# Three output-product stages of a two-layer transformer: weights staged in idle buffers, first tile evicted and multiplied between the weights' roundings

## What is computed

```python
# am, first attention layer
mixed = concat([rmsnorm(out_a, g_out_a), rmsnorm(out_b, g_out_b)])   # (1024, 1024)
x1 = x + mixed @ w_out                                             # (1024, 1024) @ (1024, 1024)
# em, retention and stick-breaking layer
mixed = concat([group_norm(ret) * silu(gate), stick * silu(gate)])
x3 = x2 + rms_norm(mixed @ even_w_out, post_norm)
# om, recurrent layer
mixed = concat([group_norm(hc) * silu(gate), lru_out])
out = x3 + rms_norm(mixed @ odd_w_out, post_norm)
```

## Time and profile before

| | |
|---|---|
| median of 3 runs | 2683.31 us (2678.47 to 2697.49) |
| the profiled execution | 2682.25 us, its span 2680.4 us |
| busy share of the span | PE 82%, PEld 68%, DVE 49%, ACT 39%, POOL 20% |
| mean granted TensorE clock | 0.899 |
| the eight weight pieces sent by SP (first and last issue) | am 700.5 to 712.6, em 1929.3 to 1954.0, om 2554.5 to 2566.6 |
| product's matmuls (first and last start) | am 725.9 to 824.6, em 1968.2 to 2066.9, om 2579.8 to 2671.3 |

### The profile page before, as it was taken

How to read it: one execution, slowest core, us unless ns; L and a number is a source line. 1 busy time by engine, 2 the same in 40 slices (tenths; PEclk the granted TensorE clock), 3 DMA queues, 4 the chain that set the end, 5 groups by cost and what they waited for, 6 DMA issues and landing times. The chain is left out here.

```text
span 2680.4 us, 34378 instructions
## 1 busy us (share of the span) xinstructions
PE 2210.9 (82%) x12244; PEld 1824.7 (68%) x12244; DVE 1314.9 (49%) x2225; ACT 1032.4 (39%) x1828; POOL 542.4 (20%) x658
## 2 busy tenths in 40 slices
PE   7996897999596699995599997688568899945658
PEld 5885897999584566663488885577557778834547
DVE  3334675555453666763632112577555434336743
ACT  3333554555331455552421100355343333246532
POOL 1003103421010212221200004234312000036622
PEclk9998998999797799998799997788879899977779
DMA  4777765321345399983833212332252442141142
GB/s 148 216 226 212 239 197 135 95 64 42 130 134 208 135 368 365 351 335 127 297 129 114 79 47 91 85 71 47 73 171 95 150 145 99 62 125 41 41 173 95
DMA packets 216721, 399.15 MB, mean 149 GB/s; under 512 B 90513, under 2 KB 111377, under 8 KB 203905
## 3 DMA queue, kind: packets, MB, share of 16 engines
q1 hardware_dynamic: 177008, 314.52, 37.1%
q10 hardware_dynamic: 28384, 61.62, 6.1%
q0 software_dynamic: 11184, 21.13, 2.2%
HBM read 300.16 MB, written 114.85 MB: 155 GB/s over the span
## 5 line engine op out<-in xcount | busy, mean ns | idle before, releaser
L78 PE MATMUL pe_acc<-pe_w,hT 128*128 128x512 f32 x960 | 222.5, 393 | 0.0
L78 PEld LDWEIGHTS pe_acc<-pe_w,hT 128*128 128x128 f32 x960 | 181.8, 190 | 37.8
L78 PE MATMUL ex_gu<-hT,ex_xT 128*128 128x512 f32 x792 | 194.4, 401 | 0.8 <-DVE hT L2321 0.8
L2321 DVE TENSOR_TENSOR hT<-ex_raw,hT 128x2048 fp32r<-128x2048 f32 x66 | 150.9, 2287 | 88.8 <-ACT hT L2292 88.8
L78 PE MATMUL pg_acc<-hT,pg_w 128*128 128x512 f32 x768 | 179.6, 395 | 8.6 <-DVE pg_w L257 8.6
L78 PEld LDWEIGHTS pg_acc<-hT,pg_w 128*128 128x128 f32 x768 | 145.2, 189 | 42.1 <-DVE pg_w L257 9.6
L78 PEld LDWEIGHTS ex_gu<-hT,ex_xT 128*128 128x128 f32 x792 | 147.5, 190 | 34.5 <-DVE hT L2321 1.2
L2292 ACT ACTIVATE hT<-ex_raw 128x2048 fp32r<-128x2048 f32 x66 | 126.2, 1914 | 42.4 <-PEq L47 23.9
L1697 PE MATMUL ab_op<-ab_v,ab_pT 128*128 128x64 f32 x1024 | 121.3, 272 | 0.0
L296 DVE COPY pe_o<-pe_acc 128x512 f32<-128x512 f32 x28 | 19.3, 691 | 206.6 <-PE pe_acc L78 206.5
L2250 PE MATMUL ex_dn<-ex_wd,ex_hT 128*128 128x512 f32 x264 | 118.7, 592 | 0.8 <-ACT ex_hT L2286 0.8
(11 more groups left out here) (461 smaller groups left out, 5056.0 us busy)
## 6 DMA issues: line engine op xcount, KB each, us to landing
ex_raw<-in_w_gate SPq DMA_DIRECT2D x33, 1024.0 KB, 7.7
ex_raw<-in_w_up SPq DMA_DIRECT2D x33, 1024.0 KB, 11.7
ex_wd<-in_w_down SPq DMA_DIRECT2D x33, 1024.0 KB, 14.2
pe_raw<-in_even_w_in SPq DMA_DIRECT2D x6, 2048.0 KB, 9.2
pg_raw<-in_odd_w_in SPq DMA_DIRECT2D x5, 2048.0 KB, 9.3
scr_q<-pa_o SPq DMA_DIRECT2D x32, 256.0 KB, 4.1
scr_k<-pa_o SPq DMA_DIRECT2D x32, 256.0 KB, 3.8
hT<-scr_k SPq DMA_DIRECT2D x16, 512.0 KB, 6.5
```

Source lines behind the costliest of these rows:

```text
L78: mm = pe.matmul(out, a(p, k), b(q, k), start=(k == 0 and i == 0), stop=(k == n - 1 and i == 2))
L2321: dve.tensor_tensor(split(s, LO)[:, :, g, :], raw[:, s % NW, g, :].rearrange("p (k n) -> p k n", k=8), split(s, HI)[:, :, g, :].bitcast(F3 ...
```

## The change

`mix_out` gets a list `pieces` of up to eight staging buffers: `raw`, then the back's two `xs`, then the back's two `z`. That gives NR = 8 in am, 6 in em (raw has two there) and 6 in om (there is no `z`). SP sends the rows of tile 0, then NR weight pieces without a wait, then the rows of tile 1, then what is left of the weights behind waits for the LO roundings. ACT evicts tile 0 between the sixth and the seventh rounding. DVE makes the LO parts of pieces 1 and 2 ahead of `dve_z(0)`, those of 3 to 5 behind it, then `dve_turn(0)`, then 6 to 8. PE multiplies tile 0's first half (24 matmuls) piece by piece as the LO parts come, with the turn of tile 0 ahead of the first piece that needs it, then turns tile 1, then the second half. In om the pieces are taken in the order 4, 5, 6, 7, 0, 1, 2, 3. The number of instructions of each kind is the same.

```diff
@@ -744,7 +744,7 @@
                     r.pe_turn(pe, t)
 
 
-def mix_out(nc, name, ident, hT, w_out, gain, front, back, nr=4):
+def mix_out(nc, name, ident, hT, w_out, gain, front, back, nr=4, order=tuple(range(8))):
 
 
 
@@ -756,9 +756,11 @@
         gcol = st.sb(name + "_g", [P, 8]) if gain is not None else None
         acc = [st.ps(f"{name}_acc{u}", [P, D]) for u in range(2)]
         gain_in, hi_ok, lo_ok, y_done, y_free = (st.sem(name + n) for n in ("_gain_in", "_whi_ok", "_wlo_ok", "_y_done", "_y_free"))
-        raw_in = [st.sem(f"{name}_raw_in{u}") for u in range(nr)]
         f = Rows(nc, st, name + "f", ident, **front)
         b = Rows(nc, st, name + "b", ident, y_psum=(lambda t: acc[t % 2][:, :], y_done, y_free), **back)
+        pieces = [buf[:, u, :] for buf, n in ((raw, nr), (b.xs, 2), (b.z, 2)) if buf is not None for u in range(n)][:8]
+        NR = len(pieces)
+        raw_in = [st.sem(f"{name}_raw_in{u}") for u in range(NR)]
         wv = tiled(w_out)
         STEPS = NT + 5
 
@@ -766,15 +768,18 @@
             @block.sync
             def _(sp):
                 f.load(sp, 0)
-                f.load(sp, 1)
                 if gain is not None:
                     for k0, v in gain:
                         sp.dma_start(gcol[:, k0:k0 + v.shape[0] // P], v.rearrange("(k p) -> p k", p=P),
                                      allow_slow_non_contiguous=True).then_inc(gain_in, 16)
-                for k in range(8):
-                    if k >= nr:
-                        sp.wait_ge(lo_ok, k - nr + 1)
-                    sp.dma_start(raw[:, k % nr, :], wv[:, k, :]).then_inc(raw_in[k % nr], 16)
+                for i, k in enumerate(order):
+                    if i == NR:
+                        f.load(sp, 1)
+                    if i >= NR:
+                        sp.wait_ge(lo_ok, i - NR + 1)
+                    sp.dma_start(pieces[i % NR], wv[:, k, :]).then_inc(raw_in[i % NR], 16)
+                if NR == 8:
+                    f.load(sp, 1)
                 b.load(sp, 0)
                 b.load(sp, 1)
                 for t in range(2, NT + 2):
@@ -795,46 +800,69 @@
 
             @block.scalar
             def _(act):
-                for s in range(STEPS):
+                def hi(i0, i1):
+                    for i in range(i0, i1):
+                        act.wait_ge(raw_in[i % NR], 16 * (i // NR + 1))
+                        act.activation(w[:, HI, order[i], :], pieces[i % NR], ACT.Copy, scale=scale(order[i])).then_inc(hi_ok, 1)
+
+                f.act_x(act, 0)
+                if gain is not None:
+                    act.wait_ge(gain_in, 16 * len(gain))
+                hi(0, 6)
+                f.act_turn(act, 0)
+                hi(6, 8)
+                f.act_x(act, 1)
+                for s in range(2, STEPS):
                     at_step(s, (b.act_y, 3, act), (f.act_turn, 1, act), (b.act_turn, 5, act), (f.act_x, 0, act), (b.act_x, 3, act))
-                    if s == 0:
-                        if gain is not None:
-                            act.wait_ge(gain_in, 16 * len(gain))
-                        for k in range(8):
-                            act.wait_ge(raw_in[k % nr], 16 * (k // nr + 1))
-                            act.activation(w[:, HI, k, :], raw[:, k % nr, :], ACT.Copy, scale=scale(k)).then_inc(hi_ok, 1)
                 b.act_end(act)
 
             @block.vector
             def _(dve):
-                for s in range(STEPS):
-                    at_step(s, (f.dve_z, 1, dve))
-                    if s == 1:
-                        if gain is not None:
-                            dve.wait_ge(gain_in, 16 * len(gain))
-                        for k in range(8):
-                            dve.wait_ge(hi_ok, k + 1)
-                            dve.scalar_tensor_tensor(out=w[:, LO, k, :], in0=raw[:, k % nr, :], scalar=scale(k),
-                                                     in1=w[:, HI, k, :].bitcast(F32), op0=ALU.mult, op1=ALU.subtract).then_inc(lo_ok, 1)
-                    at_step(s, (b.dve_z, 4, dve), (b.dve_x, 3, dve), (f.dve_turn, 1, dve), (b.dve_turn, 5, dve))
+                def lo(i0, i1):
+                    for i in range(i0, i1):
+                        k = order[i]
+                        dve.wait_ge(hi_ok, i + 1)
+                        dve.scalar_tensor_tensor(out=w[:, LO, k, :], in0=pieces[i % NR], scalar=scale(k),
+                                                 in1=w[:, HI, k, :].bitcast(F32), op0=ALU.mult, op1=ALU.subtract).then_inc(lo_ok, 1)
+
+                if gain is not None:
+                    dve.wait_ge(gain_in, 16 * len(gain))
+                lo(0, 2)
+                f.dve_z(dve, 0)
+                lo(2, 5)
+                f.dve_turn(dve, 0)
+                lo(5, 8)
+                for s in range(2, STEPS):
+                    at_step(s, (f.dve_z, 1, dve), (b.dve_z, 4, dve), (b.dve_x, 3, dve), (f.dve_turn, 1, dve), (b.dve_turn, 5, dve))
 
             @block.tensor
             def _(pe):
+                def half(pe, t, n, first):
+                    nn = slice(n * BANK, (n + 1) * BANK)
+                    for i, k in enumerate(order):
+                        if first:
+                            if k == 0:
+                                f.pe_turn(pe, 0)
+                                pe.wait_ge(f.lo_ok, 1)
+                            pe.wait_ge(lo_ok, i + 1)
+                        for j, (p, q) in enumerate(PARTS):
+                            mm = pe.matmul(acc[t % 2][:, nn], hT[:, p, k, t * P:(t + 1) * P], w[:, q, k, nn],
+                                           start=(i == 0 and j == 0), stop=(i == 7 and j == 2))
+                    return mm
+
                 def multiply(pe, t):
+                    if t == 0:
+                        return
                     pe.wait_ge(f.lo_ok, t + 1)
                     if t >= 2:
                         pe.wait_ge(y_free, t - 1)
-                    for n in range(2):
-                        nn = slice(n * BANK, (n + 1) * BANK)
-                        for k in range(8):
-                            if t == 0 and n == 0:
-                                pe.wait_ge(lo_ok, k + 1)
-                            for i, (p, q) in enumerate(PARTS):
-                                mm = pe.matmul(acc[t % 2][:, nn], hT[:, p, k, t * P:(t + 1) * P], w[:, q, k, nn],
-                                               start=(k == 0 and i == 0), stop=(k == 7 and i == 2))
-                    mm.then_inc(y_done, 1)
-
-                for s in range(STEPS):
+                    half(pe, t, 0, False)
+                    half(pe, t, 1, False).then_inc(y_done, 1)
+
+                half(pe, 0, 0, True)
+                f.pe_turn(pe, 1)
+                half(pe, 0, 1, False).then_inc(y_done, 1)
+                for s in range(3, STEPS):
                     at_step(s, (f.pe_turn, 1, pe), (b.pe_turn, 5, pe), (multiply, 2, pe))
 
 
@@ -3345,7 +3373,8 @@
     mix_out(nc, "om", ident, hT, A["odd_w_out_2"][0], None,
             dict(width=512, loads=[(0, 512, lambda t: rows(scr["hc"], t))], groups=[(128 * h, 128) for h in range(4)], hT=hT,
                  gate=[(0, 512, lambda t: rows(scr["orows"][:, 512:1024], t))]),
-            dict(width=D, loads=[(0, D, lambda t: rows(scr["x3"], t))], groups=[], post=A["post_norm_w_2"][1], keep=out))
+            dict(width=D, loads=[(0, D, lambda t: rows(scr["x3"], t))], groups=[], post=A["post_norm_w_2"][1], keep=out),
+            order=(4, 5, 6, 7, 0, 1, 2, 3))
 
 
 SCRATCH.update(erows=(S, 1536), sqkT=(1024, S), srows=(S, 1024), ret=(S, 512), stick=(S, 512), x3=(S, D),
```

## The result

The changed kernel takes 2643.78 us (median of 4 runs, 2641.96 to 2650.18) against 2688.19 for the kernel before in the runs beside it (4 runs, 2678.47 to 2697.49). The ratio is 0.986, with an interval of 0.982 to 0.990: faster by 1.4%. The profiled execution took 2643.15 us, with a span of 2641.3 us and a mean granted clock of 0.903; before it was 2682.25, 2680.4 and 0.899.

A forecast was written before the change was run, and what follows sets the result against it. From first to last product a stage is as long as PE's list, so only what stands ahead can be won: am 10.0 + em 17.3 + om 6.3 = 33.6 us off 2683.3 gives 2649.7, stated as 2649; range 2640 to 2663.

The forecast's parts named there:

- The list of events: am: first half from 715.0 to 722.5, turn 1 at 722.5, second product at 729.6 in place of 739.60.
- The new wait ahead of turn 2: em: tile 2 is ready only at 1962.8, so PE stands idle 2.5 us ahead of its turn.
- The term taken over: em: from `act_x(1)` to the turn of tile 1 takes 7.24 us, as in the trace of before.
- The gating multiply that I put on the path: em: DVE's gating multiply, formerly done while POOL worked, now stands on the path, 1.22 us.
- the 1 us taken off for the clock: em: 1 us deducted from the 18.3 us gain, since an idle of about that length can lower PE's clock.
- The early first rounding: em: first piece lands two pieces' time earlier, at 1933.1; ACT is free at 1934.0; first rounding before was 1935.65.
- The idle ahead of turn 1: om: PE idles 2.7 us between the first half's end and tile 1's turn, so the clock's rise is paid again.
- ACT's wait for the turn of tile 0: om: ACT waits for that turn with the last two roundings behind it, 2.3 us lost; in em 2.7 us.
- the early landing brings nothing: All three stages: only the halves are hidden, 3 x 5.6 = 17 us won, 2666 us; chance 0.05.
- The clock staying low: Tile 0's halves run at 1.2 GHz throughout; in em and om alone it takes 9 to 13 us, 2660; chance 0.06.
- rival 1: Chain to turn 1 not shortened: pieces 1.75 us apart, ACT's wait costing twice; 24 us won, 2659; chance 0.08.

The follow-up runs named there:

- the first run: The changed kernel as first measured and profiled, against the kernel before: 2643.78 us, ratio 0.986; em 127.0 us.
- the second: The changed kernel measured once more with no edit: 2648.82 us, ratio 0.986 to the kernel before; em 123.8 us.
- the natural order: The changed kernel, but om takes its pieces in the order 0 to 7: om 3.3 to 3.4 us shorter.
- staging alone: The changed kernel's staging buffers and SP order, with the orders of before on ACT, DVE and PE: ratio 0.992 to the kernel before.
- the combination: The changed kernel with turns amid products, om's pieces 0 to 7, tile 0's gate first and 12 warming transposes per stage: 2639.06 us, 0.984 to the kernel before.

## Why the prediction was right, point by point

The forecast was 2649 us and 33.6 us won; two profiles of either kernel show 31.1 to 35.1 in the three stages, and the median was 2643.78. The measured ratio, 0.982 to 0.990, takes in the forecast's 0.987.

**am: 10.0 forecast, 10.1 to 10.8 measured.** The list of events came as worked out: first half right after tile 0's LO eviction, turn 1 at once, turn 2 in time. One of POOL's tensor_scalars took 1.04 us there too (0.19 before), but turn 1 stands behind the first half and did not wait for it.

**em: 17.3 forecast, 15.6 and 17.6 measured, like with like.** The new wait ahead of turn 2 came as 2.48 us for 2.5. That the clock may fall in it was right as a chance: it fell in the first run and not in the second. What the prediction did not have was POOL. It took for turn 1 that "from `act_x(1)` to the turn it took 1966.55 - 1959.31 = 7.24 us" and would again; it took 1937.34 - 1928.61 = 8.7 us, with the tensor_scalars at 2.76 us in place of 1.28, so PE waits 1.33 us there. The term taken over from a stretch in which the last LO rounding had ended was mis-sized by 1.5 us, all of it the one tensor_scalar of 1.95 us for 0.47, and tile 0's roots by 1.9. The gating multiply that I put on the path was hidden behind them. That 17.3 was met all the same is in part luck: without the 1 us taken off for the clock the prediction says 18.3, and the pair in which the clock stayed up shows 17.6, so a reserve for something that did not happen there covered POOL, which it did not have; in the other pair both happened, and it is 15.6. The early first rounding came as forecast only where SP's second transfer was issued quickly.

**om: 6.3 forecast, 6.0 to 6.3 measured.** The idle ahead of turn 1 (2.16 us for 2.7) and the second half at 7.30 for 7.2 came as forecast. Turn 1 came 26.2 us after the first transfer (26.35 before), where I had it 1 us earlier: from `act_x(1)` to it 6.3 us went by in place of 5.74, POOL again (two of its tensor_scalars took 0.51 and 0.52 us). I had priced ACT's wait for the turn of tile 0 at 2.3 us, which counts only to the start of that turn; to its end my own times give 2569.5 - 2566.1 = 3.4, and it measured 2.96 and 3.19. I left it there; the natural order shows that it was worth undoing.

**The rivals.** That the early landing brings nothing fell with "staging alone" (16.4 us). The clock staying low fell: in the changed kernel every product after the first takes 11.0 to 11.2 us but em's second, which took 11.86 in one run. The second half of om runs at a mean of 0.77, as the forecast had it. Of rival 1 the effect came in part and neither cause did: the chain to turn 1 was 1.5 us longer in em and 0.6 in om, but the pieces, where ACT waited for them, followed each other at 1.27 to 1.32 us (the first two of om at 1.41 and 1.49), and ACT's wait for the turn of tile 0 in em was 2.40 and 2.45 us for 2.7.

**Outside the three stages** the first profiled pair differs by 8.0 us more, which no step of the prediction had. Two profiles of the changed kernel differ there by 12.5 us, so it may be chance, and it is open in part, as said above. The medians are 44 us apart and the ratio stands for about 38, so the total does not confirm the forecast more closely than that; the stages do.

## What to carry to other kernels

When a stage is as long as one engine's list, ask what that engine could do before its first wait ends, and then what it will wait for next: half of a tile's product, put ahead of the next tile's turn, was worth 6.5 us in am, where the next tile was ready (the half's 5.6 and part of the clock's rise), 5.2 in em and 3.5 in om, where PE then waited for the chain of four engines that brings it. A duration taken from the trace of before holds only beside the work that stood beside it there: with DVE's LO rounding and multiply beside it, a POOL instruction of 0.19 us ended only behind them, up to 1.95 us after it had begun. A mean over a group of instructions hides this; a window on one of them shows it. Compare a change inside a program of 2.6 ms by the lengths of its own stages; the untouched stretch between two of them varied by 22 us over the fourteen profiles.

## What the runs showed of the hardware that was not expected

POOL's tensor_scalar of 128x1 takes 0.19 us alone; started beside DVE's scalar_tensor_tensor or tensor_tensor of 128x1024 with both inputs in SBUF it ended 0.05 us after that instruction, in em after a multiply of the same kind that followed at once (0.47 to 1.95 us). Its power of 128x4 takes 1.03 us alone and 1.89 when its first 1.0 us lie beside a LO rounding. A wait of PE of 2.5 us behind a busy stretch is sometimes followed by the granted clock of 0.50 (1.2 GHz) and sometimes not: turn and product behind it took 1.97 and 11.86 us in one run of the same program and 1.09 and 11.17 in another; of the six profiles with that wait (2.48 to 2.50 us ahead of em's turn 2) the clock fell in four. Twelve transposes, 2.4 to 2.8 us of work that nobody uses, put into a wait ahead of a first half brought the half from 7.9 to 5.7 us in am, and did not raise the clock in time in om of the combination. And the issue of SP's second transfer in em takes 0.43 us in some runs and 1.4 to 1.8 in others, and in five of the six profiles with the slow issue ACT's first rounding began 10.1 to 11.1 us after the first transfer (8.9 in the sixth; 7.8 to 8.7 with the quick issue and the new staging); no run here shows what decides it.
